# Two products' operands converted inside attention, the last merge after the barrier, and expert weight loads that wait for gathered rows

## The reference, cut to what matters

```
yb = mla(...)                       # 16 heads of 64, chunk-causal, 1024 tokens
merged = gates[:, :, 0] * ya + gates[:, :, 1] * yb
h = h + merged @ w_out_2            # 1024 x 1024 by 1024 x 1024
u = rms_norm_2(h, norm_ffn_g)
# router: 4 groups, 8 experts in each; the best group, its two best experts
# expert e on its tokens: (silu(u @ w_gate[e]) * (u @ w_up[e])) @ w_down[e]
h = h + sum over the two experts of combine * expert(u)
```

## Time and profile before

| what | us |
|---|---|
| three runs | 2809.44, 2800.74, 2808.06 |
| median | 2808.06 |
| profiled execution | 2801.2, its span 2799.4 |
| attention's last TensorE instruction starts | 2268.86 |
| last stage starts | 2285.60 |
| first w_out_2 product | 2287.98 |
| first gather issued, its rows turned | 2417.85, 2427.07 |
| SP's last weight load (w_down) | 2741.97 |

### The profile page before, as it was taken

One profiled execution on the slowest core, in us unless ns is written; L12 is line 12 of the kernel. 1 busy time (PEld: TensorE's weight loads), 2 busy tenths in 40 slices (PEclk: granted clock), 3 DMA queues, 4 the chain that ended last, 5 costly groups with the idle time before them and its releaser, 6 DMA issues. The chain is left out here.

```text
span 2799.4 us, 32456 instructions
## 1 busy us (share of the span) xinstructions
PE 2666.6 (95%) x12208; PEld 2098.1 (75%) x12208; DVE 1643.6 (59%) x2299; ACT 1202.4 (43%) x1842; POOL 338.6 (12%) x288
## 2 busy tenths in 40 slices
PE   7999999999999999999999999899999969699997
PEld 5888888888878787777777779898666648567665
DVE  5688888888642333443333333587666642688785
ACT  4234434444340222555245242565555542356553
POOL 0010111101100000000000000034122220125332
PEclk9999999999999999999999999999999989899999
DMA  4111111111124212021221232134432122689994
GB/s 134 46 46 53 47 37 53 53 53 38 39 90 166 75 46 91 31 68 38 68 62 36 67 109 62 42 140 132 124 101 51 30 65 91 275 311 362 348 373 149
DMA packets 206572, 294.10 MB, mean 105 GB/s; under 512 B 54629, under 2 KB 162726, under 8 KB 193752
## 3 DMA queue, kind: packets, MB, share of 16 engines
q1 hardware_dynamic: 191272, 267.93, 28.1%
q0 software_dynamic: 14288, 21.06, 2.2%
q10 hardware_dynamic: 864, 3.15, 0.3%
HBM read 262.56 MB, written 58.25 MB: 115 GB/s over the span
## 5 line engine op out<-in xcount | busy, mean ns | idle before, releaser
L384 PE MATMUL PS<-UHI,WHI 128*128 128x512 f32 x1008 | 416.0, 413 | 4.1 <-DVE ULO L127 4.1
L384 PE MATMUL PS<-ULO,WHI 128*128 128x512 f32 x1008 | 400.3, 397 | 0.0
L384 PE MATMUL PS<-UHI,WLO 128*128 128x512 f32 x1008 | 400.2, 397 | 0.0
L127 DVE TENSOR_TENSOR WLO<-arena,WHI 128x1024 fp32r<-128x1024 f32 x94 | 115.3, 1227 | 215.0 <-ACT WHI L123 214.8
L384 PEld LDWEIGHTS PS<-UHI,WHI 128*128 128x128 f32 x1008 | 190.6, 189 | 52.3 <-issue 5.5
L384 PEld LDWEIGHTS PS<-ULO,WHI 128*128 128x128 f32 x1008 | 190.7, 189 | 47.6 <-issue 5.5
L384 PEld LDWEIGHTS PS<-UHI,WLO 128*128 128x128 f32 x1008 | 190.3, 189 | 46.4
L1486 PE MATMUL PS<-U2HI,WHI 128*128 128x512 f32 x480 | 193.1, 402 | 2.6 <-DVE WLO L127 2.6
L1486 PE MATMUL PS<-U2HI,WLO 128*128 128x512 f32 x480 | 189.6, 395 | 0.0
L1486 PE MATMUL PS<-U2LO,WHI 128*128 128x512 f32 x480 | 189.5, 395 | 0.0
L820 DVE SCALAR_TENSOR_TENSOR RC<-arena,cols,RC 128x1024 f32<-128x1024 f32 x120 | 157.2, 1310 | 10.3 <-issue 0.9
(11 more groups left out here) (484 smaller groups left out, 6083.3 us busy)
## 6 DMA issues: line engine op xcount, KB each, us to landing
arena<-in_w_in SPq DMA_DIRECT2D x88, 512.0 KB, 3.9
arena<-in_w_gate SPq DMA_DIRECT2D x13, 1024.0 KB, 7.6
arena<-in_w_up SPq DMA_DIRECT2D x13, 1024.0 KB, 11.4
arena<-in_w_down SPq DMA_DIRECT2D x13, 1024.0 KB, 15.0
qk_dram<-RA SPq DMA_DIRECT2D x32, 384.0 KB, 2.3
arena<-qk_dram SPq DMA_DIRECT2D x32, 384.0 KB, 4.5
arena<-in_w_out SPq DMA_DIRECT2D x32, 256.0 KB, 2.7
RB<-in_w_gate SPq DMA_DIRECT2D x7, 1024.0 KB, 7.5
```

The costliest lines, as they stand in the source:

```text
L127: return eng.tensor_tensor(dst, src, hi.bitcast(F32), ALU.subtract)
L384: last = pe.matmul(o[:, h * HALF:(h + 1) * HALF], x[:, k, :], y[:, k, h * HALF:(h + 1) * HALF], start=(k == r == 0), stop=(k == ND - 1 and ...
```

## The change

1. In attention's last head ACT splits RA slices 0 and 1 into MHI (`first_merged_hi`, after units 0 and 2) and VectorE makes MLO of them between the W8LO slices. MHI moves from the arena to RC, since the arena is full at that time. RC's place for h (x1, then h2) is taken by the arena, tiles H2.
2. The merge of the last head pair (t = 7) leaves the attention stage. Its six POOL operations and the reciprocal of half 1 are the first of POOL and VectorE in the last stage (`last_merge`). MHI 7 waits for them; MHI 2 to 6 don't. TensorE's products of k = 0 and 1 wait for nothing.
3. Weight loads 2 and 3 wait for gathers 0 and 1 to land. Load b from 5 on waits for gather b - 2 besides `down(b - 5)`. The fourth and fifth home are exchanged, and ACT waits for the stores of h2 before `upper(0)`, since GUHI 0 lies where H2 was.

```diff
+                def first_merged_hi(k):
+                    act.wait_ge(s_score, NUNIT * (NHEADS - 1))
+                    act.wait_ge(s_merged, 2 * k + 2)
+                    split_hi(act, MHI[:, k, :], RA[:, k, :]).then_inc(s_firsthi, 1)
...
+                        if h == NHEADS - 1 and k in (0, 2):
+                            first_merged_hi(k // 2)
...
-                for t in range(NPAIRS):
+                for t in range(NPAIRS - 1):
                     merge(t)
...
+                pool.wait_ge(s_sigland[(NPAIRS - 1) % 2], 16 * ((NPAIRS - 1) // 2 + 1))
...
+                    if h + 1 == NHEADS:
+                        for k in range(4):
+                            if k < NFIRST:
+                                first_merged_lo(k)
+                            merge_weights_lo(4 + k)
...
-                reciprocals(NPAIRS - 1, 1)
...
-        HOMES = ("RB", 0), ("RA", 0), ("arena", 0), ("arena", 6), ("RC", 0)
+        HOMES = ("RB", 0), ("RA", 0), ("arena", 0), ("RC", 0), ("arena", 6)
...
-                    if b < 4:
+                    if b < 2:
                         sp.wait_ge(s_h2p, NT)
+                    elif b < 4:
+                        sp.wait_ge(s_xland[b - 2], 16)
                     elif b < NRW:
                         sp.wait_ge(s_h2st, 16 * 2 * NT)
                     else:
                         sp.wait_ge(s_down, b - NRW + 1)
+                        sp.wait_ge(s_xland[(b - 2) % NBUF], 16 * ((b - 2) // NBUF) + 16)
...
-                    pe.wait_ge(s_mlo, k + 1)
+                    if k >= NFIRST:
+                        pe.wait_ge(s_mlo, k + 1 - NFIRST)
...
                 def merged_hi(k):
+                    if k == ND - 1:
+                        act.wait_ge(s_lastmerge, 2)
                     split_hi(act, MHI[:, k, :], RA[:, k, :]).then_inc(s_mhi, 1)
...
                 act.wait_ge(s_log, NT)
+                act.wait_ge(s_h2st, 16 * 2 * NT)
                 upper(0)
...
+                def last_merge(half):
+                    at = slice(half * HALF, (half + 1) * HALF)
+                    y = YB[(NPAIRS - 1) % 2][:, at]
+                    if half:
+                        pool.wait_ge(s_lastrec, 1)
+                    pool.tensor_tensor(y, y, SUMREC[half], ALU.mult)
+                    pool.drain()
+                    pool.tensor_tensor(y, y, SIG1[(NPAIRS - 1) % 2][:, at], ALU.mult)
+                    pool.drain()
+                    pool.tensor_tensor(RA[:, NPAIRS - 1, at], RA[:, NPAIRS - 1, at], y, ALU.add).then_inc(s_lastmerge, 1)
+                    pool.drain()
+
+                last_merge(0)
+                last_merge(1)
                 pool.memset(ONES[:], 1.0).then_inc(s_ones, 1)
...
-                for k in range(ND):
+                dve.reciprocal(SUMREC[1], SUMREC[1]).then_inc(s_lastrec, 1)
+                for k in range(NFIRST, ND):
                     merged_lo(k)
```

More of the change, by code:

```diff
@@ L1208, in build @@
         W8HI, W8LO = rounded("W8HI", "arena", 0, [P, ND, D]), rounded("W8LO", "RB", 0, [P, ND, D])
+        MHI, MLO = rounded("MHI", "RC", 0, [P, ND, T]), rounded("MLO", "RA", 0, [P, ND, T])
+        NFIRST = 2
         MAXHI, MAXLO = rounded("MAXHI", "arena", 8 * T, [P, P]), rounded("MAXLO", "arena", 8 * T + 128, [P, P])
@@ L1254, in build @@
         s_lss = sem("s_lss")
+        s_firsthi = sem("s_firsthi")
         s_lms = sem("s_lms")
@@ L2392, in merge_weights_lo, with first_merged_lo @@
                     split_lo(dve, W8LO[:, k, :], RB[:, k, :], W8HI[:, k, :]).then_inc(s_w8lo, 1)
+                def first_merged_lo(k):
+                    dve.wait_ge(s_firsthi, k + 1)
+                    split_lo(dve, MLO[:, k, :], RA[:, k, :], MHI[:, k, :])
                 for n in range(NTILES):
@@ L2429, in _ @@
                         features_lo(h + 2, 1)
-                    else:
+                    elif h + 2 == NHEADS:
                         for k in range(4):
-                            merge_weights_lo(4 * (h + 2 - NHEADS) + k)
-                reciprocals(NPAIRS - 1, 1)
+                            merge_weights_lo(k)
         retire(s_held)
@@ L2439, in build @@
         list_dram = nc.dram_tensor("list_dram", [NOVER * P, 3], I32).ap()
-        MHI, MLO = rounded("MHI", "arena", 8 * T, [P, ND, T]), rounded("MLO", "RA", 0, [P, ND, T])
+        H2 = [part((8 + m) * T, (T,)) for m in range(NT)]
         XNT = [part((16 + k) * T, (ND, P)) for k in range(2)]
@@ L2511, in build @@
         s_mhi = sem("s_mhi")
+        s_lastrec = sem("s_lastrec")
+        s_lastmerge = sem("s_lastmerge")
         s_mlo = sem("s_mlo")
@@ L2635, in _ @@
                     sp.wait_ge(s_h2, 2 * m + 2)
-                    sp.dma_start(h2_dram[m * P:(m + 1) * P, :], RC[:, m, :]).then_inc(s_h2st, 16)
-                    sp.dma_start(out_rows[m * P:(m + 1) * P, :], RC[:, m, :]).then_inc(s_h2st, 16)
+                    sp.dma_start(h2_dram[m * P:(m + 1) * P, :], H2[m]).then_inc(s_h2st, 16)
+                    sp.dma_start(out_rows[m * P:(m + 1) * P, :], H2[m]).then_inc(s_h2st, 16)
                 for b in range(NS):
@@ L2662, in turn_tokens @@
                         pe.wait_ge(s_xnt, m)
-                    pe_turn(pe, banks(4), RC[:, m, :], s_xnturn)
+                    pe_turn(pe, banks(4), H2[m], s_xnturn)
                 def logits(m):
@@ L2827, in root_of @@
                     act.wait_ge(s_h2, 2 * m + 2)
-                    act.activation(SQUARES[:], RC[:, m, :], ACT.Square, accum_out=sumsq[:, m:m + 1])
+                    act.activation(SQUARES[:], H2[m], ACT.Square, accum_out=sumsq[:, m:m + 1])
                     act.drain()
```

6 lines of the change are left out of this document (3 added, 3 removed).

## The result

The changed kernel takes 2789.62 us (median of 7 runs, 2785.61 to 2796.06) against 2808.06 (7 runs, 2800.74 to 2809.61) in the same comparison: a ratio of 0.9949, 95% interval 0.9938 to 0.9959, so 14 us less, with 12 to 17 inside the interval. Forecast were 2795 and 13.2 us less. The profiled execution of the changed kernel was the longest of its seven (2796.06, span 2794.2), that of the kernel before (span 2799.4) nearly the shortest; the spans differ by 5.2 us only. Part of that lies ahead of the change: VectorE's first W8LO, which nothing in the change touches, starts at 2245.05 in one trace and at 2250.05 in the other. I therefore compare distances between events.

A forecast was written before the change was run, and what follows sets the result against it. Time was seen only in TensorE's gaps (attention's end, first gathered rows) and the expert loop, where TensorE and DMA limits lie close. 11.7 + 1.5 + 0 = 13.2 us, from the median 2794.9, given as 2795; range 2783 to 2803.

The forecast's parts named there:

- The stage's start: End of attention: with the last merge moved out, the next stage starts at 2275.1, 10.5 us earlier.
- The tail: End of attention: ACT's last results come 1.1 us later because MLO 0 lengthens POOL's multiply of merge 6.
- TensorE's clock: First products of the new stage: half clock assumed, 24.8 us kept; a full-speed start would give back up to 2.5.
- the stage's first term: Attention's end and the following stage: tile 2 starts 11.7 us earlier, ends of the term 8 and 13.
- The router's loads: Start of the new stage: SP's loads end last, 24.2 us plus 0.46 for the gain, and set tile 2's start.
- The cover of the moved merge: New stage: the moved merge finishes before TensorE wants k = 7, by 2.4 us, or 5.7 with overlap.
- The start's hold: First gathered rows: holding loads 2 and 3 gains 1.5 us, VectorE's share rows then being the limit.
- all after turn 1 shifts with it: Behind the first gathered rows: TensorE's second turn and everything later move earlier by the 1.5 us gained there.
- The loop's hold: Expert loop: loads are held by what TensorE waits, 6.6 us over eight loads, without a bubble; gain 0.
- A: Expert loop: held loads free late gathers, experts go at 10.14 us, 9.8 more gained, 2785; chance 0.14.
- B: Expert loop: held loads find the weight queue empty and restart it, fifteen lose 30 us, 2825; chance 0.08.
- C: Attention's end or first gather does less than counted; about 6 us remain, 2802; chance 0.16.

The follow-up runs named there:

- e6: Changed kernel without the two early splits, all eight merged rows split behind the barrier: 2794.02 us, ratio 0.9956 to the kernel before.
- e7: Changed kernel with the router's constants loaded ahead of six of the eight x1 loads: 2787.47 us, ratio 0.9935 to the kernel before.
- e5: Changed kernel with the last pair's merge ahead of the barrier again, early splits kept: 2798.05 us, ratio 0.9979 to the kernel before.
- e11: Changed kernel with weight loads 2 and 3 held longer, until TensorE has turned block 1's rows: 2789.89 us, ratio 0.9946 to the kernel before.
- e4: Kernel before with one edit, weight loads 2 and 3 held until gathers 0 and 1 land: 2805.67 us, ratio 1.0005 to the kernel before.
- e12: Second profiled execution of the kernel before with only loads 2 and 3 held until gathers 0 and 1 land: 2807.60 us, ratio 1.0013.

## Why the prediction came out right, point by point

**The stage's start** was put 10.5 us earlier and came 11.4 earlier. The tail was 0.7 us longer where I took 1.1 (POOL's multiply 6.59 us, counted 5.46 + 1.1), and from ACT's last result to the start it was 1.6 us, not 2.1.

**TensorE's clock** was the wrong choice inside the stage's first term. I kept the 24.8 us of a k-loop that starts at half clock and named 2.5 us as the price of that. TensorE went in at full clock (0.47 us for its first product) and had done two tiles 22.6 us after the start (2304.11 less 2.34, less 2279.20). e6 shows the other side: 8.09 us of idle time, and the half clock is back.

**The router's loads** end last, as said; e7 shows it. They took 23.1 us where I took 24.2 (both to VectorE's gain), so tile 2 came 13.9 us earlier instead of 11.7. The 1.1 us go with POOL's store of the empty list, which I had left open by 1.5 us either way: with it 0.9 us behind the start, the loads took 23.2 to 24.2 us in four traces, with it 12 us behind and the same eight x1 loads ahead, 22.4 to 23.1 in eight. Since TensorE was ahead of them, the clock at the start paid nothing, as e5 shows. TensorE's wait for them, 2.34 us, was followed by a lower clock (0.89 for 15 us, 1.00 in e11 after a wait of 1.64): from tile 2 to the table it took 105.0 us, 103.7 before and 103.5 in e11. I had counted that at nothing.

**The cover of the moved merge** held. I gave it 2.4 us without overlap and, by the Trainium skill ("SBUF — State Buffer", Who interferes with whom), 5.7 with it. The trace agrees with the page: POOL's operations beside the single-input reciprocal take 1.29 to 1.30 us, those beside the two-input MLO 1.80 to 2.10. The last MLO ends with VectorE's row, at 2282.51 + 10.95 = 2293.46, and TensorE wants it at 2279.2 + 7/8 x 22.6 = 2299.0: 5.5 us.

**The start's hold** was put at 1.5 us and is 1.7, with VectorE's share rows next in line, as said; gather 0 landed 4.7 us after its issue where I took some 3. That all after turn 1 shifts with it is the weak sentence: e4 and e12 have the same 1.7 us and lose them, and more, to the clock. Here it held (24.4 us to load 5, as before); nothing in my working could have told the two apart.

**The loop's hold** was put at 0 with the right mechanism: it holds loads by what TensorE waits, 10.5 us over eleven loads (I had 6.6 over eight), and no bubble arises. The trace is 3.4 us longer, twice; without the hold a part of that remains, so 0 may be 2 us too good. The Trainium skill ("DMA: Bandwidth & Descriptors", Queues, rings and completion order) has each DMA engine take turns between queues packet by packet. The landings agree with that: gathers in the held loop land 13.1 us after issue in the median (before 12.8); only the first three, with their two loads nearly through, land after 4.7 to 5.1. No run here shows the turns themselves.

**The rivals.** A (2785, a faster loop) and B (bubbles) are out by the loop's length and by e11. C is out at attention's end. The size, 14 us for 13.2, is nearer than the terms deserve. Tile 2 came 2.2 us earlier than I said (0.9 of it the start's) and the start's hold gave 0.2 more; against them stand 1.3 us of clock behind tile 2, 3.4 in the loop and 0.7 behind load 32, all of which I had at nothing. In the traces that leaves 10.2 us. That the forecast lies between these 10.2 and the ratio's 14 is in part luck.

## What to carry to other kernels

When work is moved behind a barrier, what starts with the barrier can become the bound: list the stage's first loads in the order in which they are needed, small constants ahead of bulk rows (3.0 us here). A gather that others wait for lands in half the time if the bulk loads that would be queued ahead of it are held until it has landed (4.7 us for 9.2), but where its queue stays full anyway, a hold only delays loads. A microsecond won in front of a starved TensorE can be lost again to its clock a few microseconds later (1.7 won, 4.6 lost in e4 and e12), so look at the granted clock behind the place, not at the wait alone.

## What the hardware showed that I had not expected

- The clock behind a starved stretch can turn a gain round, and repeatably: in the kernel before with the second turn 1.7 us earlier, a gap of 2.08 us was followed by 14 us at 0.63 to 0.64, and load 5 came 4.6 us later behind that turn, in two executions out of two. In e6 a gap of 2.25 us at the same place, between the same products, was followed by 1.00. What decides is open.
- SP's issue of the router's group weights takes 0.89 us behind two x1 loads, 4.68 to 6.21 behind eight (eight traces), and 10.7 to 11.6 behind the same eight where POOL's store of the empty list (24 KB) is issued 0.9 us behind the stage's start (four traces: before, e4, e12, e5). Most of such an issue, then, isn't a price of its own; that it waits for what is queued ahead is how I read it. That the small store slows the x1 loads (12.0 and 11.8 us to landing against 7.4) rests on e5 beside the changed kernel: the store is the one DMA whose place among them differs.
- Three gathers issued within 3.2 us land after 4.7 to 5.1 us when two loads precede them, and after 9.2, 11.7 and 14.2 us when five do.
